# A pooled/attention/MoE block on one core: the end of the expert loop is written out, and constants are multiplied while the router is awaited

## The reference, cut to what matters

```
x += concat([attention(h), pool(h)]) @ W_out
x += memory_cross_attention(rmsnorm(x))
h  = rmsnorm(x)
g  = argmax(h @ Wg)                       # one of 4 groups
top 2 of the 8 experts of g, gates = softmax(g)[g] * softmax(top2)
out[t] = x[t] + sum over its 2 experts e of
         gate * ((silu(h[t] @ w_gate[e]) * (h[t] @ w_up[e])) @ w_down[e])
```

## Time and profile before

| what | value |
|---|---|
| median of three runs | 1718.97 us |
| profiled execution, its own time | 1719.06 us |
| its span (first to last instruction) | 1717.3 us |
| mean granted TensorE clock | 0.984 |
| PE / DVE / ACT / POOL busy | 91% / 36% / 19% / 9% |
| HBM read, over the span | 484.81 MB, 287 GB/s |
| share of the last chain: PE / DMA / DVE / ACT | 66% / 20% / 8% / 3% |
| longest wait of PE | for DMA of expert weights, 58.6 us in 48 times |

### The profile page before, as it was taken

One profiled execution on the slowest core, in us unless ns is written; L12 is line 12 of the kernel. 1 busy time (PEld: TensorE's weight loads), 2 busy tenths in 40 slices (PEclk: granted clock), 3 DMA queues, 4 the chain that ended last, 5 costly groups with the idle time before them and its releaser, 6 DMA issues.

```text
span 1717.3 us, 18475 instructions
## 1 busy us (share of the span) xinstructions
PE 1560.7 (91%) x7036; PEld 859.3 (50%) x7036; DVE 612.9 (36%) x755; ACT 334.5 (19%) x600; POOL 152.2 (9%) x225
## 2 busy tenths in 40 slices
PE   6999999989999898789999899889889889989997
PEld 5587777758887445534343333333334333333433
DVE  3455656652223323423233222313213323231333
ACT  4322334342221234210101010010011101001010
POOL 1470045510000000000000000000000000000000
PEclk9999999999999999789999999999999999999999
DMA  7433222342216030579999999999999999999994
GB/s 271 123 87 85 79 69 74 124 153 97 92 57 252 18 123 25 235 284 422 419 421 422 422 422 422 421 421 422 421 422 421 422 421 421 422 421 420 420 421 189
DMA packets 115049, 484.40 MB, mean 282 GB/s; under 512 B 9427, under 2 KB 47421, under 8 KB 62141
## 3 DMA queue, kind: packets, MB, share of 16 engines
q1 hardware_dynamic: 111008, 470.84, 68.5%
q0 software_dynamic: 3264, 12.88, 2.0%
q10 hardware_dynamic: 732, 0.07, 0.0%
HBM read 484.81 MB, written 8.39 MB: 287 GB/s over the span
## 4 chain that ended last, share of the span: by engine, by line
PE 66%; DMA 20%; DVE 8%; ACT 3%; issue 2%; ACTq 0%; SPq 0%; DVEq 0%; POOLq 0%
DMA weight_ring<-in_expert_w_up_dram 20%; PE ps L1925 18%; PE ps L1667 10%; PE ps L1545 8%; PE ps L1953 8%; PE ps L1776 3%; PE ps L1903 3%; PE ps L1720 3%; DVE residual L1427 3%; PE ps L1904 2%; PE ps L1496 2%; PE ps L1507 2%; ACT weight_ring L761 1%; DVE w_in_low L1031 1%; PE ps L1802 1%
## 5 line engine op out<-in xcount | busy, mean ns | idle before, releaser
L1925 PE MATMUL ps<-weight_ring,transposed_acts 128*64 128x512 f32 x2016 | 462.0, 597 | 59.4 <-DMA weight_ring<-in_expert_w_up_dram 58.6
L1925 PEld LDWEIGHTS ps<-weight_ring,transposed_acts 128*64 128x64 f32 x2016 | 150.4, 137 | 365.2 <-issue 255.4
L1953 PE MATMUL ps<-weight_ring,transposed_acts 128*64 128x512 f32 x1024 | 226.8, 595 | 18.9 <-DVE transposed_acts L1434 18.9
L1427 DVE TENSOR_TENSOR residual<-ps,residual 128x1024 f32<-128x1024 f32 x128 | 151.1, 1221 | 252.0 <-PE ps L1904 251.1
L1445 DVE SCALAR_TENSOR_TENSOR y_low<-ps,proj_buffer,y_high 64x1024 fp32r<-64x1024 f32 x64 | 82.1, 1283 | 211.1 <-ACT y_high L932 210.1
L1953 PEld LDWEIGHTS ps<-weight_ring,transposed_acts 128*64 128x64 f32 x1024 | 71.7, 137 | 155.3 <-issue 151.3
L932 ACT ACTIVATE y_high<-ps,proj_buffer 64x1024 fp32r<-64x1024 f32 x64 | 71.0, 1109 | 306.1 <-PE ps L1953 305.3
L1903 PE MATMUL ps<-y_high,spread 128*128 128x512 f32 x256 | 113.9, 445 | 14.3 <-DVE residual L1427 10.3
L1545 PE MATMUL ps<-mix_high,w_in_high 128*128 128x512 f32 x288 | 116.6, 405 | 1.3 <-issue 1.3
L1545 PE MATMUL ps<-mix_high,w_in_low 128*128 128x512 f32 x288 | 112.3, 390 | 0.0
L1545 PE MATMUL ps<-normed_low,w_in_high 128*128 128x512 f32 x288 | 112.3, 390 | 0.0
(11 more groups left out here) (265 smaller groups left out, 1691.8 us busy)
## 6 DMA issues: line engine op xcount, KB each, us to landing
weight_ring<-in_expert_w_down_dram SPq DMA_DIRECT2D x128, 1024.0 KB, 19.0
weight_ring<-in_expert_w_gate_dram SPq DMA_DIRECT2D x126, 1024.0 KB, 23.6
weight_ring<-in_expert_w_up_dram SPq DMA_DIRECT2D x126, 1024.0 KB, 25.6
weight_ring<-in_w_in_dram SPq DMA_DIRECT2D x18, 1024.0 KB, 5.7
weight_ring<-in_w_out_dram SPq DMA_DIRECT2D x16, 1024.0 KB, 5.1
weight_ring<-in_xkv_w_dram SPq DMA_DIRECT2D x8, 1024.0 KB, 6.4
residual<-in_x_dram SPq DMA_DIRECT2D x8, 1024.0 KB, 15.7
weight_ring<-in_xq_w_dram SPq DMA_DIRECT2D x4, 1024.0 KB, 9.1
```

What stands on the lines that cost most here:

```text
L1427: v.tensor_tensor(part, ps[:, bank:bank + 2, :].rearrange("p b n -> p (b n)"), part, ALU.add).then_inc(sum_ready if last else part_added, 1)
L1925: ins = mm(ps[side * SLOTS:(side + 1) * SLOTS, 0, :], xsT[:, k, par * SLOTS:(par + 1) * SLOTS], expert_weights(b, j, kk), start=(k == 0), ...
L1953: ins = mm(ps[half, 4 + n // 2, :], act_t[:, f * SLOTS:(f + 1) * SLOTS], w[:, n * 512:(n + 1) * 512], start=(f == 0), stop=(f == KF - 1), ...
```

## The change

1. **The last pair is written out** (`last_blocks` on PE and DVE, two calls of `block_act` on ACT). The loops stop one pair earlier, and the reading of the number of further blocks with both `If`s now stands between block 29 and block 30. In blocks 30 and 31 only parts 3, 4 and 5, 6 of pair 28/29 are spread. Block 31 has no row turning and DVE no copy of turned rows. Parts 0, 1, 2 are spread after block 31's down product into bank pairs 6, 2, 0 and left open; the same parts of the last pair are accumulated onto them. Part 7 carries both pairs too; parts 3 to 6 only the last pair. Three bank pairs rotate.
2. **Own tiles for the last pair**: `last_hi`, `last_lo`, `last_spread`, in room that is free by then. The one-hot `last_spread` is made before block 30.
3. **Column halves.** Column block n goes to partition half n // 2 and bank 4 + n % 2, in the order 0, 2, 1, 3. A half of y is then a half of the columns. Part i is tile i % 4, column half i // 4; the first four parts of the last pair wait for one half of y only.
4. **Stores of half tiles**: eight of 128 x 1024 (512 KB), each after one add.
5. **Products of constants** (`keep_busy(n)`: n products of ones by the identity, 128 x 128 x 128 f32, into bank 7, read by nobody): 10 after the last logits, 14 after the ranks, 4 after the token table, 8 after the gate table.

```diff
@@ SP
-            for t in range(NT):
-                sp.wait_ge(sum_ready, 2 * t + 2)
-                sp.dma_start(out[0, t * P:(t + 1) * P, :], X[:, t, :]).then_inc(stored, 16)
+            for i in range(2 * NT):
+                t, side = part_of(i)          # i % NT, i // NT
+                sp.wait_ge(sum_ready, i + 1)
+                sp.dma_start(out[0, t * P:(t + 1) * P, side * 1024:(side + 1) * 1024], ...
@@ ACT
-            with act.Fori(1, NE // 2) as it:
+            with act.Fori(1, NE // 2 - 1) as it:
...
+            with act.If(more < 1):
+                block_act(NE - 2, 0, last_hi)
+                block_act(NE - 1, 1, last_hi)
@@ DVE
+            def last_blocks():
+                b, added = NE - 2, 4 * NE - 16
+                v.tensor_scalar(last_spread[:, :], tramp, tokf[:, b:b + 1], None, ALU.is_equal).then_inc(spread_ready, 1)
+                for par in range(2):
+                    gated(b + par)
+                    add_part_of(3 + 2 * par, 6, added + 2 * par + 1, part_added)
+                    add_part_of(4 + 2 * par, 2, added + 2 * par + 2, part_added)
+                    for side in range(2):
+                        y_rest(b + par, par, side, last_hi, last_lo)
+                for i in range(2 * NT):
+                    add_part_of(i, LAST_BANKS[i % 3], added + 4 + i + 1, sum_ready)
@@ PE
+            def keep_busy(n):
+                for _ in range(n):
+                    mm(ps[:, 7, 0:P], ones[:, :], ident[:, :], start=True, stop=True)
+            keep_busy(10)      # then the wait for the picks, ranks
+            keep_busy(14)      # then the wait for the one-hots, token table
+            keep_busy(4)       # then the wait for the gates, gate table
+            keep_busy(8)       # then turn_rows(0)
@@ PE, down product
-                    for n in range(4):
-                        half = slice(n % 2 * SLOTS, (n % 2 + 1) * SLOTS)
-                        ins = mm(ps[half, 4 + n // 2, :], ...
+                    for n in (0, 2, 1, 3):
+                        half = slice(n // 2 * SLOTS, (n // 2 + 1) * SLOTS)
+                        ins = mm(ps[half, 4 + n % 2, :], ...
@@ PE
+            def last_blocks():
+                b, added = NE - 2, 4 * NE - 16
+                for par in range(2):
+                    gate_up(b + par, par)
+                    if par == 0:
+                        pe.wait_ge(y_dve, 2 * b)
+                        pe.wait_ge(spread_ready, b // 2)
+                    pe.wait_ge(part_added, added + 2 * par - 1)
+                    spread_matmuls(3 + 2 * par, 6, spread, y_hi, y_lo).then_inc(part_done, 1)
+                    turn_gu(b + par)
+                    pe.wait_ge(part_added, added + 2 * par)
+                    spread_matmuls(4 + 2 * par, 2, spread, y_hi, y_lo).then_inc(part_done, 1)
+                    down(b + par)
+                for i in range(3):
+                    if i < 2:
+                        pe.wait_ge(part_added, added + 3 + i)
+                    spread_matmuls(i, LAST_BANKS[i], spread, y_hi, y_lo, stop=False)
+                pe.wait_ge(spread_ready, b // 2 + 1)
+                for i in range(2 * NT):
+                    side = part_of(i)[1]
+                    if i >= 3:
+                        pe.wait_ge(sum_ready, i - 2)
+                    if i == 7:
+                        spread_matmuls(i, LAST_BANKS[i % 3], spread, y_hi, y_lo, stop=False)
+                    if i % NT == 0:
+                        pe.wait_ge(y_dve, 2 * b + 2 + side + 1)
+                    spread_matmuls(i, LAST_BANKS[i % 3], last_spread, last_hi, last_lo,
+                                   start=(3 <= i < 7)).then_inc(part_done, 1)
```

More of the change, by code:

```diff
@@ L931, in block_act @@
                     rows = slice(side * SLOTS, (side + 1) * SLOTS)
-                    a.activation(y_hi[par * SLOTS:(par + 1) * SLOTS, side:4:2, :], ps[rows, 4:6, :], ACT.Copy,
+                    a.activation(high[par * SLOTS:(par + 1) * SLOTS, 2 * side:2 * side + 2, :], ps[rows, 4:6, :], ACT.Copy,
                                  scale=gate[rows, ds(b, 1)]).then_inc(y_act, 1)
@@ L1467, in _ @@
             with dve.If(more < 1):
-                for half in range(2):
-                    add_parts(4 * NE - 8, half, last=True)
+                last_blocks()
         @block.tensor
@@ L1889, in expert_weights, with spread_matmuls @@
                 return slot(expert_slot(j)).rearrange("p (k n) -> p k n", n=FF)[:, kk, :]
+            def spread_matmuls(i, bank, onehot, high, low, start=True, stop=True):
+                t, side = part_of(i)
+                for y in (high, low):
+                    for n in range(2):
+                        ins = mm(ps[:, bank + n, :], onehot[:, t * P:(t + 1) * P], y[:, 2 * side + n, :],
+                                 start=(start and y is high), stop=(stop and y is low))
+                return ins
             def spread_parts(before, half, last=False):
                 for i in range(4 * half, 4 * half + 4):
-                    t = i // 2
                     if i >= 2:
@@ L1900, in spread_parts @@
                             pe.wait_ge(part_added, before + (i - 1))
-                    for n in range(2):
-                        bank, cols_ = (6, 2)[i % 2] + n, 2 * (i % 2) + n
-                        mm(ps[:, bank, :], spread[:, t * P:(t + 1) * P], y_hi[:, cols_, :], start=True, stop=False)
-                        ins = mm(ps[:, bank, :], spread[:, t * P:(t + 1) * P], y_lo[:, cols_, :], start=False, stop=True)
-                    ins.then_inc(part_done, 1)
+                    spread_matmuls(i, (6, 2)[i % 2], spread, y_hi, y_lo).then_inc(part_done, 1)
             def last_pair(blocks):
@@ L1928, in block_pe, with turn_gu, down @@
                                 ins.then_inc(used, 1)
+            def turn_gu(b):
+                pe.wait_ge(gu_copied, b + 1)
+                for f in range(KF):
+                    ins = turn(guT[:, f, :], gu[:, f * P:(f + 1) * P], ident[:, :])
+                ins.then_inc(gu_turned, 1)
+            def down(b):
+                pe.wait_ge(act_ready, b + 1)
+                wait_past(pe, y_dve, b * 2)
+                for f in range(KF):
+                    expert_landed(b, 8 + f)
+                    w = slot(expert_slot(8 + f))
+                    for n in (0, 2, 1, 3):
+                        half = slice(n // 2 * SLOTS, (n // 2 + 1) * SLOTS)
+                        ins = mm(ps[half, 4 + n % 2, :], act_t[:, f * SLOTS:(f + 1) * SLOTS],
+                                 w[:, n * 512:(n + 1) * 512], start=(f == 0), stop=(f == KF - 1), skip_group_check=True)
+                    ins.then_inc(used, 1)
+            def block_pe(b, par, pair):
+                gate_up(b, par)
                 if par == 1:
@@ L1938, in block_pe @@
                     spread_parts(pair * 8 - 8, 0)
[L1939 to L1942 removed]
+                turn_gu(b)
                 if behind:
                     spread_parts(pair * 8 - 8, 1)
[L1945 to L1955 removed]
+                down(b)
```

77 lines of the change are left out of this document (41 added, 36 removed).

## The result

Five runs of the changed kernel took 1705.87 to 1710.62 us, median **1706.98**, beside 1718.02 (1713.28 to 1720.56) of five of the kernel before: ratio 0.9942 [0.9922, 0.9961] (in brackets, here and below, the 95% interval of the ratio). That is 11.0 us less, where 10.2 were forecast. Run again later, twelve runs gave a median of 1708.83 and 0.9949 [0.9932, 0.9966].

What follows compares the result with a forecast made beforehand. The prediction took a saturated stream of expert weights (421 GB/s, 920 of 1717 us) to bound the kernel, leaving only its start and end to gain. 1719.06 - 6.2 (end) - 4.0 (start) = 1708.9 us, range 1705.8 to 1713.4.

Steps and rivals of the forecast that it cites:

- likeliest case: The whole kernel: the forecast itself, 1708.9 us, own range 1707 to 1711, chance 57%.
- part 6: Start: products of constants in PE's waits bring back the clock, weight stream starts earlier; 4.0 us, bounds -1.1 and 5.3.
- Part 1 and 2: Blocks 30 and 31: less spreading, no unused turning; block 31's down product starts 1.8 us earlier in all.
- Part 3: Wait for y in the tail: PE fills it with spreading; DVE adds at once, where it waited 2.17 us.
- Part 4: Tail sums: eight adds, about 1.15 us each without waits, ending at 1707.5 instead of 1713.0; gain 5.5 us.
- Part 5: Eight 512 KB stores: their queue sets the end, 11.7 us after first issue; gain at the end 6.2 us.
- Rival C: Tail stores: half stores are slow, following each other at 2.0 us; 1714.9 us, chance 8%.
- Part 7: Taken branch moved ahead of block 30: 3.74 us on PE, free up to 14 us, counted as nothing.
- Rival D: Branch ahead of block 30: its fetch queues like a weight, 26.1 us; 1723.5 us, chance 4%.
- Rival B: Start: the clock is not held, products give only -1.1 to 1.5 us; 1712.5 us, chance 26%.

Runs made afterwards that it cites:

- the two with more products: Changed kernel plus seven products of constants in and behind the logits, the second also with 6 instead of 8 in the last group: 1706.36 and 1707.10 us.
- tail only: Changed kernel without the four groups of products of constants: median 1712.17 us, ratio to the kernel before 0.9970.
- clock of the tail: Kernel before plus 14 products of constants on PE between block 31's down product and the wait for y: median 1716.08 us, ratio 0.9993.

## Why the prediction was right, and where its terms were off

**Right in mechanism, and in its sum partly by luck**: 1708.9 forecast, 1706.98 measured, inside the range and 0.02 us below the likeliest case's own range of 1707 to 1711. The sum fits better than its terms: what part 6 named gave 2.9 us of its 4.0, and 2.4 us came from what it had taken as nothing or not seen. Without the part not seen, 1.66 us, A, B and C together would have given 9.4 us, still close to the 10.2.

- *Part 1 and 2, block 31.* PE waits for DMA up to the last chunk. Landing to down product 6.2 us, 6.05 in the prediction's terms (1681.05 to 1687.1). Held.
- *Part 3, y.* Filled, full clock, first add 17.2 us behind the landing as predicted. Making it wait for both halves, and giving only the clock, split it: 1.2 us for the halves, 1.7 for the clock.
- *Part 4, sums.* Last add 5.6 us earlier against the landing, 5.5 predicted.
- *Part 5, stores.* Issue to end 12.10 instead of 11.7: 0.4 us too little. They land 1.29 us apart, while 1.26 was taken from the rate of 1 MB stores, and a store alone takes 2.6 us. So C gave 5.73 instead of 6.2. Rival C (2.0 us apart) is out. The Trainium skill (DMA: Bandwidth & Descriptors, section Bandwidth) asks for at least 1 MiB a transfer to get 75% of peak, from a table measured on loads; the 406 GB/s of queued 512 KB stores do not agree with it, and the measurement decides here.
- *Part 6, products.* The mis-sized term: 4.0 predicted, 5.87 - 0.57 = 5.3 in the trace, at the upper bound, but not from the terms that were added up. Turning to gate-and-up gave 1.13 (1.7 predicted: at full clock DVE's scaling copies pace it, 1.36 us idle behind L1432). First release gave 2.33 (2.55). The gather was issued 13.71 instead of 14.46 us behind the logits, 0.75: the table products, taken as nothing. The remaining 1.66 is the gather's landing, 4.3 us instead of 6.0, which the prediction did not have at all. B cost 0.57 instead of 0.25, a difference that B's scatter doesn't let one read. So the named terms gave 1.13 + 2.33 - 0.57 = 2.9.
- *Part 7, branch.* It took 6.12 us, not 3.74, held PE idle for 3.07 and was followed by 3.4 us of half clock, and all of it was covered. The predicted cover of 14 us was right (14.5, counted the same way). Rival D needed 22 to 24 us: out.
- *Rival B*, that the clock is not held, did not come true: in the nine traces with four groups of products the turning takes 1.97 to 2.07 us and block 0's gate-and-up 13.95 to 13.96. The clock is low in each somewhere, in the changed kernel from about 722 to 725, in its second profile and in the two with more products also in block 0's down product (8.79 us instead of 7.09), but never where block 0 releases its first slots. Where it is low in that down product B is longer: 934.23 to 935.27 us in those three, 932.90 to 933.69 in the other six. So some of what the products gain in A is at times lost again in B. That down product, in the second profile of the changed kernel:

```profile
760.64 8.79 PE L1995 MATMUL ps<-weight_ring,transposed_acts 128*64 128x512 f32 x32 [1.49 <-DVE transposed_acts L1452]
```

**What the medians say of the size.** The products gave 5.7 us of A in a profile but 3.4 by medians. Two things in the traces point that way. In three of the nine with all four groups B is longer, as just told. And one of the three kernels with no products of constants ahead of block 0 (before, tail only, clock of the tail) recovered its clock by itself (A 28.08 instead of 30.92 and 31.00). Averaged over these nine and three traces A + B is 959.2 and 963.1 us: 3.9 us apart, between the medians' 3.4 and the prediction's 4.0. Three traces are few, so this is a likely reason and not a shown one.

## What to carry to other kernels

Read a wait of TensorE twice: as lost time, and by the clock of what follows. At the start, filling the waits shortened none of them by itself, and the clock of what follows still gave about 3.5 us; at the end it gave 1.7. Fill with real work moved from elsewhere if there is some, with products of constants if not, and see that the filling is shorter than the wait at the lower clock too. Where a stream bounds the middle, work out how late the engine may be at the stream's end (here 14 us, by adding up the blocks behind it), and put every unavoidable stall, such as a taken branch, inside that slack.

## What the runs showed of the hardware

**A transfer lands later where an instruction fetch falls into it.** The instruction queue moves one packet of 16 KB now and then. DMA view of the 6.2 us behind the issue of block 0's gather, in the kernel without the first two groups and then in the one without the last two:

```profile
q8 instruction: 1, 0.02, 1.8%
...
proj_buffer<-normed_rows,slot_columns POOLq DMA_INDIRECT x1, 5.8
```

```profile
q0 software_dynamic: 144, 0.42, 24.8%
...
proj_buffer<-normed_rows,slot_columns POOLq DMA_INDIRECT x1, 4.4
```

The second has no q8 row. Over the 14 traces, the four with such a packet in this window have the gather landing after 5.7 to 6.1 us (before: 6.0), the ten without after 4.2 to 5.0 (nine of them 4.2 to 4.4). The trace has the landing of each of a transfer's 16 pieces. In three of the four, 15 pieces are down by 4.4 us, as elsewhere, and one alone comes at 5.8 to 6.1; in the fourth (tail only) the last two come at 5.0 and 5.7. A packet is not the only thing that can hold a piece back: the gather of 5.0 us has one late piece too and no packet. And the four are just the four kernels without the first 24 products, so the gathers alone don't tell the packet from whatever else these products shift. The stores show the same in other kernels:

```profile
q8 instruction: 1, 0.02, 0.7%
...
out_dram<-residual SPq DMA_DIRECT2D x8, 512.0 KB, 4.7
```

That is the kernel with 20 products before block 30. It and the tail-only kernel are the two whose packet falls into the stores, and they took 13.44 and 13.42 us from first issue to end, where the other eight kernels with these eight stores took 12.09 to 12.12. The delay starts with the packet: in the kernel with 20 products it starts at 1698.96, the first store has landed after 2.69 us as elsewhere, the second (issued 1697.81) has 15 pieces down by 2.85 us and the last at 3.94, and so it stays to the eighth, 5.09 instead of 3.75. So the unforeseen 1.66 us of part 6 go with the place of the fetch: the 24 products ahead moved it to 724.9, before the gather was issued at 729.78, while before it was at 735.3, inside (731.58 to 737.53). No run moved the fetch alone, so this is a split of 24 awaited transfers and no experiment. The Trainium skill (Runtime: NRT & Kernel Launch, Instruction fetch mechanics) says that instructions are refilled in 16 KiB blocks by DMA and that crossing a block is mostly hidden; here the size agrees, and where a packet fell into a transfer that was awaited, it landed 1.3 to 1.9 us later.

**A taken branch took longer where the DMA was full.** 3.6 to 3.7 us in the three traces where it lay beside the last down product, 6.0 to 6.3 in the eleven where it lay in the stream. An instruction packet starts 1.0 us into the branch in the kernel before and 3.6 us into it in the changed one (1693.7, branch at 1692.7; 1630.4, branch at 1626.8), so the added time lies ahead of the packet. The branch stands at another place of the program in the two groups, and no run tells that from the full DMA.

**The clock can fall on a TensorE that was busy without a gap.** With 36-column products it fell in the logits of most traces, at different points; 32 records then took 6.88 us instead of 3.66 to 4.08. The end of the logits lies 9.4 us apart (712.64 and 722.07) in two kernels whose code is the same up to there, the tail-only one and the changed one in its second profile, as much as whole runs of one kernel scatter.
